# One stage for the mLSTM steps and the output projection, weight loads moved in the first stage, and a norm by a diagonal product

## The chip, the cores and the metric

One core of one Trainium2 chip. The time is the device time of one execution in microseconds; before the change the median of 3 runs is 1603.19 us (1601.73 to 1606.86). TensorE (PE) multiplies, VectorE (DVE), ScalarE (ACT) and GpSimd (POOL) do elementwise work, and SyncE (SP) issues the DMAs. A matmul keeps a stationary operand in the array, streams a moving operand past it and writes a bank of PSUM (8 banks of 512 f32 per partition).

## The reference, cut to what matters

One layer on 1024 prompt rows and 8 streams of 16 sample rows, 1152 rows of 1024 numbers in all:

```python
h = _rmsnorm(x, norm1)
gq, gk, gv, gr, glr, mq, mk, mv, mo, mi, mf = _split_proj(h @ w_in)
o_g = _head_rmsnorm(gla(gq, gk, gv, log_a), gla_norm) * silu(gr)      # 4 heads: half "a" of the mix
h_m = _head_rmsnorm(sigmoid(mo) * mlstm(mq, mk, mv, i, log_f), m_norm) # 4 heads: half "b" of the mix
x = x + concat([o_g, h_m]) @ w_out
y, conv_new = _conv_ffn(_rmsnorm(x, norm2), conv_st, w_g, w_u, conv_w, conv_b, w_d)
x = _rmsnorm(x + y, norm_f)
# _mlstm per chunk: num = qk@v + w*(q@C); den likewise; h = num/den; C = decay*C + k^T v (a recurrence over chunks)
```

## The kernel before

Rows go in 9 tiles of 128; the sample rows are tile 8. Large products are split in three: each f32 operand is written as hi + lo (f32r), and `mm3` (lines 91 to 95) adds hi*hi, lo*hi and hi*lo in one bank. ACT writes a weight's hi part by a copy, POOL its lo part by a subtraction; a weight comes in pieces of 128x1024 (512 KB). There are four stages, each with its own semaphores and a barrier behind it:

- `front` (0 to 494.7 us): norm 1, the input projection, and the GLA steps. `front_order` writes the order of the work out by hand, and every engine walks the same list: ("w", i) splits piece i, ("t", ...) and ("n", ...) are projection groups whose results go to DRAM, ("score", s), ("out", s), ("load", s) are a GLA step. Each projection group and GLA bank takes the next of 4 PSUM banks in a ring, and waits until that bank was emptied. SP issues in list order too: at ("w", i) it loads piece i + 2 into one of two raw slots, as soon as piece i is split, and every store and load behind it in the list waits along with it. `load` 2 brings the gate rows (`grin`, line 509) that DVE needs in `out` 2.
- `memory` (494.7 to 619): 8 prompt steps and then the sample step of the mLSTM. Per step PE transposes columns, multiplies q by k, then (when DVE has weighted that, `m_am`) the numerators, and the updates of the state C; DVE divides, and writes C; ACT sums squares. The step's inputs are loaded two steps ahead. The state makes each step wait for the one before. The halves of the mix go unscaled into `x9` (the GLA half loaded from DRAM, the mLSTM half by DVE).
- `output` (619 to 766.2): all head norms at once (`scale`, line 1468, on DVE and POOL), PE transposes of the mix (`Turn`, line 120), products with the 8 pieces of w_out, the residual added by DVE, and norm 2 (`Norm`: squares on ACT, a scaled copy `o_x_scaled` by DVE at line 185, transposed by PE at line 120). The transposed, normalised rows stay in `h2T_hi` and `h2T_lo`.
- `ffn` (766.2 to 1602.2): 11 pairs of 128 FFN columns, PE idle only before its first product and behind its last.

These lines say what a step before waits for:

```python
            def two_on(c, s):
                for n in ("am_ready", "qs_ready", "kt_ready"):
                    sp.wait_ge(g[n], c + 1)
                front(c + 2, s)
```

## Time and profile before

| | us |
|---|---|
| median of 3 runs | 1603.19 |
| the profiled execution | 1604.1 |
| its span | 1602.2 |
| PE busy | 1490.3 (93%) |
| DVE, ACT, POOL busy | 608.0, 438.7, 426.4 |
| mean granted clock of PE, share of full | 0.956 |

The span runs from the first to the last instruction. PEclk is the share of full speed that the clock throttle granted PE. A bracket behind a timeline row tells how long the engine was idle before it, and for whom it waited. SPq rows are DMA issues, not transfers. `m_` names belong to the mLSTM stage, `o_` to the output stage, `f_` to the FFN, `p_` to the first; `bank` is PSUM.

### The profile page before, as it was taken

How to read it: one execution, taken by the hardware profiler on the slowest of the kernel's cores; microseconds unless marked ns; L12 is line 12 of the kernel's file. 1: busy time of each engine (PE TensorE's matmuls, PEld its weight loads, DVE VectorE, ACT ScalarE, POOL GpSimd, SP SyncE). 2: the span in 40 equal slices, each digit the busy share in tenths (PEclk: the TensorE clock that was granted, in tenths of full speed). 3: DMA queues.
4: the chain of work that ended last, by engine and by line, in shares of the span. 5: the costliest groups of instructions: out<-in, count | busy, mean ns of one | idle time of the engine just before them, and what ended most of it. 6: DMA issues, size and time to landing. Idle time of an engine off the chain costs nothing.

```text
span 1602.2 us, 20822 instructions
## 1 busy us (share of the span) xinstructions
PE 1490.3 (93%) x7946; PEld 1359.7 (85%) x7946; DVE 608.0 (38%) x1189; ACT 438.7 (27%) x892; POOL 426.4 (27%) x356
## 2 busy tenths in 40 slices
PE   5999999989995785998899999999999999999997
PEld 5988878879995675776899898989899999989896
DVE  6352302545621436133233424243433333342426
ACT  5222222323311333132422131322232222213123
POOL 2312224254311223300431322313241313132220
PEclk9999999989996766999899999999999999999999
DMA  5312433232226733320210101111111101010103
GB/s 192 127 53 95 155 108 116 83 104 89 80 68 213 207 95 119 119 79 0 85 53 26 52 27 51 39 39 52 37 44 37 65 26 52 26 52 26 39 13 123
DMA packets 69329, 122.97 MB, mean 77 GB/s; under 512 B 5440, under 2 KB 40836, under 8 KB 68640
## 3 DMA queue, kind: packets, MB, share of 16 engines
q1 hardware_dynamic: 69280, 122.31, 22.7%
q8 instruction: 31, 0.51, 0.1%
q14 instruction: 18, 0.15, 0.0%
HBM read 93.65 MB, written 28.64 MB: 76 GB/s over the span
## 4 chain that ended last, share of the span: by engine, by line
PE 51%; DVE 1%; POOL 0%; ACT 0%; issue 0%; POOLq 0%
PE bank L93 17%; PE bank L94 17%; PE bank L95 17%; DVE x L1831 1%; DVE x L1812 0%; POOL f_w_lo L1670 0%; ACT f_w_hi L1692 0%; DVE f_inv L1824 0%; DVE f_ss L1822 0%; ACT f_rstd L1735 0%; POOLq L1663 0%; POOLq L1665 0%; POOLq L88 0%
## 5 line engine op out<-in xcount | busy, mean ns | idle before, releaser
L93 PE MATMUL bank<-h2T_hi,f_w_hi 128*128 128x384 f32 x1056 | 354.1, 335 | 6.7 <-POOL f_w_lo L1670 6.7
L94 PE MATMUL bank<-h2T_lo,f_w_hi 128*128 128x384 f32 x1056 | 353.9, 335 | 0.0
L95 PE MATMUL bank<-h2T_hi,f_w_lo 128*128 128x384 f32 x1056 | 353.8, 335 | 0.0
L1681 POOL TENSOR_TENSOR f_a_lo<-f_gate_conv,f_a_hi 128x384 fp32r<-128x384 f32 x66 | 67.0, 1015 | 579.9 <-ACT f_a_hi L1721 579.9
L93 PEld LDWEIGHTS bank<-h2T_hi,f_w_hi 128*128 128x128 f32 x1056 | 199.1, 189 | 7.4 <-POOL f_w_lo L1670 7.0
L94 PEld LDWEIGHTS bank<-h2T_lo,f_w_hi 128*128 128x128 f32 x1056 | 199.1, 189 | 0.4
L95 PEld LDWEIGHTS bank<-h2T_hi,f_w_lo 128*128 128x128 f32 x1056 | 199.1, 189 | 0.0
L1812 DVE TENSOR_TENSOR x<-bank,x 128x512 f32<-128x512 f32 x198 | 136.8, 691 | 126.0 <-PE bank L95 126.0
L1670 POOL TENSOR_TENSOR f_w_lo<-w_raw,f_w_hi 128x1024 fp32r<-128x1024 f32 x66 | 157.5, 2394 | 0.8 <-ACT f_w_hi L1692 0.8
L93 PE MATMUL bank<-f_w_hi,f_a_hi 128*128 128x512 f32 x396 | 154.4, 390 | 0.3
L95 PE MATMUL bank<-f_w_hi,f_a_lo 128*128 128x512 f32 x396 | 154.3, 390 | 0.0
L94 PE MATMUL bank<-f_w_lo,f_a_hi 128*128 128x512 f32 x396 | 154.3, 390 | 0.0
L1794 DVE TENSOR_SCALAR f_gate_conv<-f_gate_prompt,f_taps 128x384 f32<-128x384 f32 (+1 forms) x66 | 31.2, 473 | 298.2 <-ACT f_gate_prompt L1707 203.4
L93 PE MATMUL bank<-p_w_hi,p_h1T_hi 128*128 128x512 f32 x288 | 112.6, 391 | 3.6 <-POOL p_w_lo L545 3.6
L95 PE MATMUL bank<-p_w_hi,p_h1T_lo 128*128 128x512 f32 x288 | 112.1, 389 | 0.0
L94 PE MATMUL bank<-p_w_lo,p_h1T_hi 128*128 128x512 f32 x288 | 112.1, 389 | 0.0
L93 PE MATMUL bank<-p_h1T_hi,p_w_hi 128*128 128x384 f32 x312 | 106.7, 342 | 3.4 <-DVE p_h1T_lo L892 3.4
L545 POOL TENSOR_TENSOR p_w_lo<-p_raw,p_w_hi 128x1024 fp32r<-128x1024 f32 x29 | 69.8, 2413 | 148.5 <-ACT p_w_hi L601 148.3
L94 PE MATMUL bank<-p_h1T_lo,p_w_hi 128*128 128x384 f32 x312 | 105.7, 339 | 0.0
L95 PE MATMUL bank<-p_h1T_hi,p_w_lo 128*128 128x384 f32 x312 | 105.6, 338 | 0.0
L93 PEld LDWEIGHTS bank<-f_w_hi,f_a_hi 128*128 128x128 f32 x396 | 74.3, 188 | 16.9 <-DVE x L1812 1.6
L95 PEld LDWEIGHTS bank<-f_w_hi,f_a_lo 128*128 128x128 f32 x396 | 74.3, 188 | 15.5
(201 smaller groups left out, 2157.0 us busy)
## 6 DMA issues: line engine op xcount, KB each, us to landing
w_raw<-in_w SPq DMA_DIRECT2D x74, 512.0 KB, 3.3
p_raw<-in_w SPq DMA_DIRECT2D x29, 512.0 KB
scratch_pN<-p_n_out SPq DMA_DIRECT2D x36, 256.0 KB, 2.0
scratch_pT<-p_t_out SPq DMA_DIRECT2D x36, 192.0 KB, 1.9
p_arena<-in_x SPq DMA_DIRECT2D x9, 512.0 KB, 7.9
p_arena<-scratch_pN SPq DMA_DIRECT2D x18, 256.0 KB, 3.0
m_t_in<-scratch_pT SPq DMA_DIRECT2D x9, 512.0 KB
x<-in_x SPq DMA_DIRECT2D x9, 512.0 KB, 4.7
```

The lines of the kernel that those rows point to most:

```text
L93: pe.matmul(out, stat[0], mov[0], start=start, stop=False)
L94: pe.matmul(out, stat[0], mov[1], start=False, stop=False)
L95: return pe.matmul(out, stat[1], mov[0], start=False, stop=stop)
L545: pool.tensor_tensor(w_lo[:, i % NS_, :], raw[:, i % 2, :], w_hi[:, i % NS_, :].bitcast(F32), ALU.subtract).then_inc(g["piece_split"], 1)
L1670: pool.tensor_tensor(w_lo[:, unit, :], raw[:, slot, :], w_hi[:, unit, :].bitcast(F32), ALU.subtract).then_inc(piece_split, 1)
L1681: pool.tensor_tensor(a_lo[:, q, s], gc[:, n % 2, :], a_hi[:, q, s].bitcast(F32), ALU.subtract).then_inc(a_split, 1)
L1794: ins = dve.tensor_scalar(dst, src(2), tap[2], tap[3], ALU.mult, ALU.add)
L1812: dve.tensor_tensor(x, bank[6 + half], x, ALU.add).then_inc(down_added, 1)
L1831: dve.scalar_tensor_tensor(out=x9[:, r, :], in0=x9[:, r, :], scalar=rstd[:, r:r + 1], in1=raw[:, 0, :], op0=ALU.mult, op1=ALU.mult).then_i ...
```

## The change

The stages `memory` and `output` become one, `back`, over 9 steps, the sample tile first. Every step's head norm, transposes and products are done as soon as its inputs are there: ("a", s, half) adds the GLA half's product of step s to a 512-column half of x, ("b", s, half) the mLSTM half's; "a" runs one or two steps ahead. `back_order` is walked by every engine, and all 8 banks are one ring. POOL scales both halves and takes inverse roots by a power; the 9 tiles of x are loaded at the stage's start. The pieces of w_out 0 to 4 are split at the end of `front`, into the places of spent ones, and 5 to 7 and the FFN's first three in `back`. In `front` the load of a piece is an item of its own ("l", i), later in the list than before. Norm 2 has no scaled copy: the FFN stage multiplies x's 128x128 blocks as stationary operand by a diagonal matrix of inverse roots (f32), which transposes and scales at once; 36 of the 72 blocks before its first product, 36 between the first ones. (In `HALVES` the blocks of 3 row tiles are named by row block and column blocks.)

```diff
--- before.py
+++ after.py
...
-        front(nc, a, o, const, cols, ssq, pb, bank)
+        front(nc, a, o, const, cols, ssq, w, raw, pb, bank)
         x9 = sb("x9", [P, RT, D])
-        memory(nc, a, o, ident, x9, ssq, pb, bank)
-        hT = [sb(f"h2T_{n}", [P, KD, ROWS], F32R) for n in ("hi", "lo")]
-        raw = sb("w_raw2", [P, 4, PIECE])
-        output(nc, a, x9, ssq, cols, hT, ident, bank, raw)
-        ffn(nc, a, o, x9, hT, bank, raw)
+        back(nc, a, o, ident, cols, ssq, ssn, rstd2, w, raw, x9, bank)
+        ffn(nc, a, o, ident, cols, rstd2, w, raw, x9, bank)
...
-           + [PC_T + t for t in range(4, NT)])
+           + [PC_T + t for t in range(4, NT)] + [PC_OUT + j for j in range(5)])
+OUT_UNIT = W_ORDER.index(PC_OUT) % N_UNITS_W
+FFN_EARLY = 3
...
+    where = {i: sum(1 for x in order[:order.index(("w", i))] if x in units) for i in range(N_UNITS_W)}
+    before = [[] for _ in range(len(units) + 1)]
+    for i in range(N_UNITS_W, len(W_ORDER)):
+        n = last_use[i - N_UNITS_W]
+        shared = units[n][0] == "n" and (W_ORDER[i - N_UNITS_W] - PC_N) % 4 < 3
+        where[i] = min(max(n if shared else n + 1, where[i - 2] + 2, where[i - 1]), len(units))
+    for i in range(2, len(W_ORDER)):
+        before[min(where[i - 2] + (1 if i > 6 else 0), len(units))].append(("l", i))
+    for i in range(N_UNITS_W, len(W_ORDER)):
+        before[where[i]].append(("w", i))
...
-                if x[0] == "w" and x[1] + 2 < len(W_ORDER):
-                    load(x[1] + 2)
+                if x[0] == "l":
+                    load(x[1])
...
+def back_order():
+
+    dense = []
+    for s in range(RT):
+        dense += [[("a", s, 0)], [("a", s, 1)] + ([("turn_a", s + 2)] if s + 2 < RT else [])]
+    take = lambda n: [x for unit in [dense.pop(0) for _ in range(n)] for x in unit]
+    order = [("load", 0), ("load", 1), ("rows", 0), ("qk", 0), ("turn_a", 0), ("turn_a", 1)] + take(2)
+    order += [("w", 5), ("w", 6), ("num", 0)]
+    for b in range(NB):
+        order += [("um", 0, b)]
+        if b == 3:
+            order += [("w", 7), ("rows", 1), ("qk", 1)]
+    order += [("load", 2)] + take(2) + [("turn_b", 0)]
+    for s in range(1, RT):
+        order += [("num", s), ("um", s, 0)]
+        if s + 1 < RT:
+            order += [("rows", s + 1)]
+        order += [("b", s - 1, 0)]
+        if s + 1 < RT:
+            order += [("qk", s + 1)]
+        order += [("b", s - 1, 1)]
+        order += take(2) if dense else []
+        order += [("load", s + 2)] if s + 2 < RT else []
+        order += [("turn_b", s)]
+    order += [("ffn", m) for m in range(FFN_EARLY)] + [("b", RT - 1, 0), ("b", RT - 1, 1)]
+    return order
...
+            def load_step(s):
+                c, slot = GLA_STEPS[s], s % 2
                 r = slice(c * P, (c + 1) * P)
...
+                if s >= 2:
+                    wait_taken(sp, last_um(s - 2))
+                sp.dma_start(rin[:, slot, :, :], a["rows"][:, :, r]).then_inc(rows_in[slot], 16)
                 for dst, q in ((wt, 0), (wq, 2)):
...
+                    sp.dma_start(dst[:, slot, :, :], a["rows"][:, q, r].unsqueeze(0).to_broadcast([P, H, P]))\
+                      .then_inc(rows_in[slot], 16)
+                sp.dma_start(tin[:, slot, :, :], a["pT"][4:NT, :, r].rearrange("t p f -> p t f"))\
+                  .then_inc(tiles_in[slot], 16)
+                sp.dma_start(vin[:, slot, :, 0:DH], a["pN"][1, c].rearrange("p (h v) -> p h v", h=H))\
+                  .then_inc(v_in[slot], 16)
+                sp.dma_start(oin[:, slot, :], a["pN"][3, c]).then_inc(v_in[slot], 16)
+            def load_og(s):
+                sp.dma_start(ogin[:, s % 2, :], a["pN"][2, GLA_STEPS[s]]).then_inc(og_in[s % 2], 16)
...
+            load_step(0)
+            sp.dma_start(caus[:, 0:P], a["const"][:, C_CAUS:C_CAUS + P]).then_inc(g["const_in"], 16)
+            sp.dma_start(caus[:, P:3 * P], a["const"][:, C_ONE:C_ONE + 2 * P]).then_inc(g["const_in"], 16)
+            sp.dma_start(parity[:, :], a["const"][:, C_PARITY:C_PARITY + 2]).then_inc(g["const_in"], 16)
+            load_og(0)
+            load_og(1)
+            load_x(0)
+            sp.dma_start(C_s[:, :, :, :], a["s_mc"]).then_inc(g["state_in"], 16)
+            load_piece(0)
+            load_x(1)
+            load_piece(1)
+            load_step(1)
+            for s in range(2, RT):
+                load_x(s)
+            for x in order:
+                if x[0] == "turn_a" and x[1] + 2 < RT:
+                    wait_filled(sp, x)
+                    load_og(x[1] + 2)
+                elif x[0] == "load" and x[1] >= 2:
+                    load_step(x[1])
+                    if x[1] == 2:
+                        sp.dma_start(o["q_mc"], C_s[:, :, :, :]).then_inc(g["state_out"], 16)
+                elif x[0] in ("w", "ffn") and piece_at(x) + 2 < len(BW):
+                    load_piece(piece_at(x) + 2)
+            for n in range(2):
+                sp.wait_ge(g["piece_split"], len(BW) - 1 + n)
+                m = FFN_EARLY + (len(BW) + n) % 2
+                sp.dma_start(raw[:, (len(BW) + n) % 2, :], a["w"][PC_FFN + m]).then_inc(g["next_in"], 16)
...
+            def scale(x, rstd):
+                x = x.rearrange("p (h v) -> p h v", h=H)
+                return pool.tensor_tensor(x, x, rstd.unsqueeze(2).to_broadcast([P, H, P]), ALU.mult)
+
+            for x in order:
+                name, s = x[0], x[1]
+                if name == "load" and s == 0:
+                    masks(0)
+                elif name == "turn_a":
+                    if s == 0:
+                        pool.wait_ge(g["roots_a"], 1)
+                    pool.wait_ge(og_in[s % 2], 16 * (s // 2 + 1))
+                    scale(ogin[:, s % 2, :], rstd_a[:, GLA_STEPS[s], :]).then_inc(g["scaled_a"], 1)
+                elif name == "num":
+                    if s + 1 < RT:
+                        masks(s + 1)
+                    c = GLA_STEPS[s]
+                    pool.wait_ge(g["squared"], s + 1)
+                    pool.tensor_scalar(ssq[:, c, H:], ssq[:, c, H:], 1.0 / P, EPS, ALU.mult, ALU.add)\
+                        .then_inc(g["roots_step"], 1)
+                    pool.wait_ge(g["roots_step"], s + 2)
+                    pool.tensor_tensor(rstd_b[:, c, :], ssq[:, c, H:], power[:, 0:H], ALU.pow).then_inc(g["roots_b"], 1)
+                    pool.wait_ge(g["roots_b"], s + 1)
+                    scale(hm[:, s % 2, :], rstd_b[:, c, :]).then_inc(g["scaled_b"], 1)
...
+            def product(x, mix, turned, k0):
+                _, s, half = x
+                out = enter(x)
+                wait_taken(pe, (turned, s))
+                for k in range(H):
+                    j = k0 + k
+                    if s == 0 and half == 0 and j >= 5:
+                        pe.wait_ge(g["piece_split"], j - 4)
+                    stat = [y[:, s % 2, k, :] for y in mix]
+                    mov = [unit(j, y)[:, half * 512:(half + 1) * 512] for y in range(2)]
+                    mm = mm3(pe, out, stat, mov, k == 0, k == H - 1)
+                mm.then_inc(g["filled"], 1)
...
+            def turn(rb, ks):
+                if ks[0] == 0:
+                    pe.wait_ge(diag_ready, rb * JR + JR)
+                for k in ks:
+                    n = rb * KD + k
+                    if rb:
+                        pe.wait_ge(lo_done, n - 3)
+                    for j in range(JR):
+                        r = rb * JR + j
+                        t = pe.matmul(turn_bank(rb, k)[:, j * P:(j + 1) * P], x9[:, r, k * P:(k + 1) * P],
+                                      diag[:, r, :], start=True, stop=True)
+                    t.then_inc(turned, 1)
...
+                            if first and m == 0:
+                                pe.wait_ge(lo_done, KD * (rb + 1))
+                            up(i, q, rb, m)
+                            if first and rb < 2 and (rb, m) != (1, 1):
+                                turn(*HALVES[2 + 2 * rb + m])
...
+            turn(*HALVES[0])
+            turn(*HALVES[1])
+            pairs(pe, body)
```

The three places that matter below, in the order that the programs have. On SP in `front`, where pieces 25 to 28 are loaded (`p_raw`, `w_raw`), before:

```order
L440 DMA p_raw<-in_w 128x1024 x3
L478 DMA scratch_pN<-p_n_out 128x512
L440 DMA p_raw<-in_w 128x1024
L473 DMA scratch_pT<-p_t_out 128x384
L506 DMA scratch_pN<-p_arena 128x512
L509 DMA p_arena<-scratch_pN 128x512
```

and after:

```order
L491 DMA scratch_pN<-p_n_out 128x512 x3
L453 DMA w_raw<-in_w 128x1024 x2
L486 DMA scratch_pT<-p_t_out 128x384
L519 DMA scratch_pN<-p_arena 128x512
L522 DMA p_arena<-scratch_pN 128x512
L466 DMA p_arena<-scratch_pN 128x512
```

Two of four piece loads, and the waits that go with them, no longer stand ahead of the gate rows' load (L509 before, L522 after).

On PE, one mLSTM step before (updates of C, then the next step's q by k, columns, transposed keys, then its numerators):

```order
L1324 MATMUL bank4<-m_v_in,m_ks 128x129 x4
L1276 MATMUL bank2<-m_t_in 128x128 x4
L1282 MATMUL bank0<-ident,m_r_in 128x4 x3
L1283 MATMUL bank0<-m_dg,m_const 128x4
L1286 MATMUL bank2<-ident,m_t_in 128x128 x4
L1310 MATMUL bank6<-m_C_prompt,m_qs 128x129
L1311 MATMUL bank6<-m_v_in,m_am 128x129
```

and the same place after (the triple at L93 to L95 comes four times in each of the step's four half products):

```order
L1489 MATMUL bank0<-m_v_in,m_ks 128x129 x4
L1435 MATMUL bank2<-ident,m_r_in 128x4 x3
L1436 MATMUL bank2<-m_dg,m_caus 128x4
L1441 MATMUL bank2<-ident,m_t_in 128x128 x4
L93 MATMUL bank4<-w_hi,m_mix_b_hi 128x512
L94 MATMUL bank4<-w_lo,m_mix_b_hi 128x512
L95 MATMUL bank4<-w_hi,m_mix_b_lo 128x512
```

48 product matmuls of 512 columns now lie between one step's updates and the next step's numerators, 12 of them before q by k.

On SP at the start of `back` (from the sample state's load; `m_og_in` is the GLA half of a step, and the last row holds those of steps 2, 3 and 4):

```order
L1266 DMA m_C_sample<-in_s_mc 128x4128
L1234 DMA w_raw<-in_w 128x1024
L1256 DMA x<-in_x 128x1024
L1234 DMA w_raw<-in_w 128x1024
L1241 DMA m_r_in<-scratch_rows 4x5x128
L1243 DMA m_wt<-scratch_rows 128x4x128
L1243 DMA m_wq<-scratch_rows 128x4x128
L1245 DMA m_t_in<-scratch_pT 128x8x128
L1247 DMA m_v_in<-scratch_pN 128x4x128
L1249 DMA m_o_in<-scratch_pN 128x512
L1256 DMA x<-in_x 128x1024 x7
L1252 DMA m_og_in<-scratch_pN 128x512 x3
```

In the stage before, SP issued two steps' inputs, the state, nine loads of 256 KB (the GLA halves, into x), and then the third step's inputs:

```order
L1194 DMA m_C_sample<-in_s_mc 128x4128
L1196 DMA x<-scratch_pN 128x512 x9
L1172 DMA m_t_in<-scratch_pT 128x8x128
L1173 DMA m_r_in<-scratch_rows 4x5x128
L1175 DMA m_wt<-scratch_rows 128x4x128
```

The seven late tiles of x (512 KB each) now stand between step 1's inputs and the GLA half of step 2.

And on the same queue from step 1 on, after:

```order
L1252 DMA m_og_in<-scratch_pN 128x512
L1241 DMA m_r_in<-scratch_rows 4x5x128
L1243 DMA m_wt<-scratch_rows 128x4x128
L1243 DMA m_wq<-scratch_rows 128x4x128
L1245 DMA m_t_in<-scratch_pT 128x8x128
```

A step's inputs are behind an `m_og_in` load, which waits until PE has filled a transpose ("turn_a").

## Rows read from the trace of the kernel before

**Rows 1.** Busy time by stretch: length, each engine's busy us, PEclk, DMA share, GB/s
```profile
0.00:494.70 494.70, 460.00 (x2506) 405.94 (x2506) 193.51 (x359) 146.87 (x268) 150.35 (x193) 0.98 0.31 104
494.70:619.00 124.30, 85.31 (x508) 78.58 (x508) 46.12 (x184) 31.48 (x145) 25.30 (x21) 0.65 0.57 177
619.00:766.20 147.20, 122.07 (x576) 100.61 (x576) 58.16 (x91) 45.42 (x79) 28.37 (x9) 0.94 0.20 72
766.20:1602.20 836.00, 822.87 (x4356) 774.56 (x4356) 310.23 (x555) 214.89 (x400) 222.38 (x133) 0.99 0.14 46
```

**Rows 2.** Waits of PE from 494 to 770.5 us: us in total, times, longest
```profile
PE bank L1310 <- DVE m_am L1360: 17.8, 8, 4.2
PE bank L1276 <- DMA m_wq<-scratch_rows: 16.2, 2, 14.5
PE bank L120 <- DVE x L1468: 11.8, 1, 11.8
PE bank L93 <- POOL f_w_lo L1670: 6.7, 1, 6.7
```

**Rows 3.** Timeline of POOL and DVE, 618 to 640 us
```profile
620.67 2.93 POOL L1468 TENSOR_TENSOR x<-x,o_rstd 128x1024 f32<-128x1024 f32 x1 [36.13 <-ACT o_rstd L1487]
627.93 2.37 POOL L1476 TENSOR_TENSOR o_w_lo<-w_raw,o_w_hi 128x1024 fp32r<-128x1024 f32 x1 [4.33 <-ACT o_w_hi L1483]
631.69 8.90 POOL L1476 TENSOR_TENSOR o_w_lo<-w_raw,o_w_hi 128x1024 fp32r<-128x1024 f32 x1 [1.39 <-ACT o_w_hi L1483]
...
631.51 6.89 DVE L1468 TENSOR_TENSOR x<-x,o_rstd 128x1024 f32<-128x1024 f32 x6
```

**Rows 4.** DMA from 506 to 526 us: all, and one issue (KB, us to landing)
```profile
DMA packets 5486, 6.73 MB, mean 337 GB/s; under 512 B 282, under 2 KB 4050, under 8 KB 5356
...
m_C_sample<-in_s_mc SPq DMA_DIRECT2D x1, 2064.0 KB, 10.2
```

**Rows 5.** Stretches of PE: in a product of 512 columns, and the sample's numerators
```profile
719.50:724.50 5.00, 5.00 (x23) 1.00 0.03 13
593.00:599.40 6.40, 6.36 (x73) 0.58 0.00 0
```

**Rows 6.** Timeline of DVE: two updates of the sample state
```profile
601.34 2.15 DVE L1389 SCALAR_TENSOR_TENSOR m_C_sample<-m_C_sample,m_col,bank 128x129 f32<-128x129 f32 x8
```

**Rows 7.** Timeline of PE in an mLSTM step
```profile
546.63 0.39 PE L1310 MATMUL bank<-m_C_prompt,m_qs 128*128 128x129 f32 x2
...
547.08 1.06 PE L1324 MATMUL bank<-m_v_in,m_ks 128*128 128x129 f32 x8
```

**Rows 8.** Timeline of SP and POOL: the last load of an mLSTM step, and its landing
```profile
537.04 0.51 SPq L1175 DMA_DIRECT2D m_wq<-scratch_rows  x1
...
541.80 1.26 POOL L1218 TENSOR_TENSOR m_wt<-m_wt,m_const 128x512 f32<-128x512 f32 x1 [6.49 <-DMA m_wq<-scratch_rows]
```

**Rows 9.** Timeline of PE: start us, us, engine line op [idle before <-releaser]
```profile
335.39 0.70 PE L826 MATMUL bank<-p_arena 64*128 64x128 f32 x2 [2.67 <-ACT p_n_out L700]
...
348.07 2.08 PE L779 MATMUL bank<-p_arena 128*128 128x256 f32 x4 [5.15 <-DVE p_arena L1040]
349.94 2.77 PE L772 MATMUL bank<-p_arena 128*128 128x128 f32 x12
...
396.06 1.03 PE L779 MATMUL bank<-p_arena 128*128 128x256 f32 x4
```

**Rows 10.** Stretches behind the FFN's first product at 770.2 us
```profile
770.00:773.00 3.00, 2.80 (x9) 2.80 (x10) 0.00 (x0) 0.00 (x0) 3.00 (x3) 0.50 0.55 175
...
776.00:779.00 3.00, 3.00 (x19) 3.00 (x19) 0.00 (x0) 1.66 (x2) 1.15 (x1) 1.00 0.70 229
```

**Rows 11.** The page, DMA issues: KB each, median us to landing
```profile
w_raw<-in_w SPq DMA_DIRECT2D x74, 512.0 KB, 3.3
```

**Rows 12.** Timeline of SP, the queue of the DMA issues, 330 to 342 us
```profile
330.57 7.06 SPq L440 DMA_DIRECT2D p_raw<-in_w  x3
...
341.16 0.43 SPq L509 DMA_DIRECT2D p_arena<-scratch_pN  x1
```

More of the change, by code:

```diff
@@ L1104, in _, with back_entries, back @@
                     take_outputs(x[1])
-def memory(nc, a, o, ident, x9, ssq, pb, bank):
-    SLOTS = 2
-    C0 = 4
+def back_order():
[23 more added lines that the diff above has]
+    return order
+def back_entries(order):
+    out = []
+    for x in order:
+        if x[0] in ("a", "b", "turn_a", "turn_b", "qk"):
+            out.append((x, "dve"))
+        elif x[0] == "rows":
+            out += [(x, "dve"), (("kt", x[1]), "act")]
+        elif x[0] in ("num", "um"):
+            out += [(x + (i,), "dve") for i in range(2)]
+    return out
+def back(nc, a, o, ident, cols, ssq, ssn, rstd2, w, raw, x9, bank):
+    order = back_order()
+    ring = Ring(back_entries(order), bank)
     with ExitStack() as ctx:
@@ new lines, in back, with wait_taken, wait_filled @@
+        last_um = lambda s: ("um", s, (NB if s == 0 else 1) - 1, 1)
+        block = ctx.enter_context(nc.Block())
+        def wait_taken(eng, name):
+            owner, n = ring.taken(name)
+            eng.wait_ge(taken[owner], n)
+        def wait_filled(eng, name):
+            eng.wait_ge(g["filled"], ring.filled(name))
+        g["filled"] = sem("filled")
+        turns = [x for x in order if x[0] in ("turn_a", "turn_b")]
+        BW = [5, 6, 7] + [PC_FFN - PC_OUT + m for m in range(FFN_EARLY)]
@@ L1289, in from_states, with enter @@
[L1289 to L1301 removed]
+            def enter(name):
+                before = ring.before(name)
+                if before:
+                    pe.wait_ge(taken[before[0]], before[1])
+                return ring.bank(name)
@@ new lines, in _ @@
+            pe.wait_ge(g["cleared"], CLEARED)
+            for x in order:
+                name = x[0]
+                if name == "rows":
+                    rows(x[1])
+                elif name == "qk":
+                    products(x[1])
+                elif name == "num":
+                    numbers(x[1])
+                elif name == "um":
+                    updates(x[1], x[2])
+                elif name == "turn_a":
+                    turn(x, ogin, "scaled_a")
+                elif name == "turn_b":
+                    turn(x, hm, "scaled_b")
+                elif name == "a":
+                    product(x, mix_a, "turn_a", 0)
+                elif name == "b":
+                    product(x, mix_b, "turn_b", H)
@@ L1400, in masks @@
                 q.then_inc(g["qm_ready"], 1)
-            def front(v, c, s):
-                diagonal(v, c, s)
-                columns(v, c, s)
-                weights(v, c, s)
-            def step(vb, vf, c, s):
-                diagonal(vf, c + 1, 1 - s)
-                hidden(vb, c, s)
-                states(vb, c, s)
-                columns(vf, c + 1, 1 - s)
-                weights(vf, c + 1, 1 - s)
-                if vf.sample:
-                    masks(c + 1, 1 - s)
-            def back(v, c, s):
-                hidden(v, c, s)
-                states(v, c, s)
@@ L1595, in ffn @@
+def ffn(nc, a, o, ident, cols, rstd2, w, raw2, x9, bank):
     NP = NF // 2
```

772 lines of the change are left out of this document (361 added, 411 removed).

## The prediction

> **What bounds the kernel now.** I read busy time by stretch first [rows 1]. In `front` and in the FFN TensorE is busy 93% and 98% of the time at a clock near full, so little can be won there. In `memory` it is busy 85.3 of 124.3 us at a mean granted clock of 0.65, and in `output` 122.1 of 147.2: 64 idle microseconds, and much of the busy time at 1.2 GHz instead of 2.4. The waits say why [rows 2]: 16.2 us for a step's inputs, 14.5 of them at the stage's start; 17.8 us in eight waits for `m_am`, a chain over ACT and DVE in every step with nothing beside it; 11.8 us from the end of `memory` over a barrier and the scaling to the first transpose; 6.7 us before the FFN's first product. The work of `memory` is a chain, that of `output` is dense: the change puts one beside the other.
>
> The sum is made against the profiled execution, 1604.1 us with a span of 1602.2, which is 0.9 above the median of 1603.19. What it replaces runs from 494.7 us (SP's first load of `memory`) to 770.2 (the FFN's first product): 275.5 us. I price the new path between the same two events, stretch by stretch, in TensorE's order.
>
> **Opening of `back`: 41 us.** Until the GLA half of step 2 is there, TensorE has transposes of steps 0 and 1 and one step's products, 24 matmuls. Those are over at about +30. The inputs land near +12: before it was +9.7, SP now waits a good microsecond for POOL's clearing, and the masks stand behind more loads. POOL's two mask operations, sample keys and two scalings of 512 columns (half of 2.93 us each, [rows 3]) take until +20, the products 8 to 10 us at the low clock. Then PE, POOL and ACT all have "turn_a" of step 2 ahead of the sample's numerators. Its load stands behind all that the order shows: two steps' inputs (1546 KB each), constants 193, two GLA halves 512, the state 2064, two pieces 1024, nine tiles of x 4608, together 11.5 thousand KB or 11.8 MB. At the measured mean of 337 GB/s [rows 4] that is 35 us; with 3 to 4 us of start, the half itself and its scaling, the transpose starts at +41. This takes loads of one queue to land about in issue order; the state's 10.2 us to landing, for 6 us of data at that rate, with two steps' loads just issued, is such a backlog. Bounds: +30 if the small load passes the others, +48 at 280 GB/s.
>
> **Sample step: 26 us.** Numerators 6.3 us, as at 593 to 599.3, mean clock 0.58 [rows 5]; DVE's division and eight state updates, 8 x 1.08 [rows 6], 11 together, since with eight banks TensorE need not wait for DVE after each; columns and weights of step 1 on DVE 2 to 3, and the rest of step 1's products some 6 us later. DVE and the low clock set this; 20 to 30.
>
> **Seven full steps: 117 us.** At full clock a 512-column matmul comes every 0.227 us (22 periods in 5 us, [rows 5]), an mLSTM product in two passes every 0.225 (two in 0.45, [rows 7]). Per step: 48 x 0.227 = 10.9, numerators 8 x 0.225 = 1.8, updates 0.9, q by k 0.9, columns and keys 1.4, two rounds of transposes 1.0: 16.9 us. Seven are 118, less 1 for two that have one round. The chains are covered: in `memory` all of DVE's work is 46.12 / 9 = 5.1 us a step, ACT's 3.5, POOL's 2.8 [rows 1]; even all three and a scaling of 1.5 end to end are 13, and TensorE has 15 us of other work between numerators and "turn_b". So the 17.8 us go, and what is late next is a load.
>
> **Late inputs: 23 us.** From step 1 on SP loads a step's inputs behind an `m_og_in` load that waits for a "turn_a" of PE. That transpose is the last thing but one of a step, and the next step needs the inputs for its columns after only 3.2 us (turn_b, numerators, updates). From the issue of the last of them, `m_wq`, to POOL's start it took 4.8 us [rows 8]; with the other load, rows and wt issued ahead (1.7 us) and the keys' 512 KB behind them, the transposed keys start at about +9: 9 - 3.2 - 0.6 = 5.2 us lost. Queued behind them is all else of PE's step. SP waits so for "turn_a" 4, 5 and 6, ahead of loads 3, 4 and 5; later loads have no such wait. Three times 5.2 is 15.6. A wait of 2.67 us was enough to bring the clock down [rows 9]: at 348 us four 256-column matmuls took 2.08 us against 1.03 at 396. From 770.2 the clock was at half for the first 3 us, full from 776 [rows 10]: some 5 us of work at half speed, so 2.5 us for each wait, 7.5. Bounds 0 (loads land in 3 us) and 40 (every step).
>
> **Last step 9, tail 16, opening of the FFN 12.5.** Step 8 has numerators 1.8, updates 0.9, half products of step 7 5.4, turn_b and its wait 0.9: 9. From there PE needs 7 us for its last products, but the weights take longer: ACT and POOL split the pieces ffn 0, 1, 2 only now, 2.4 us each on POOL [rows 3], the third is loaded once the first is split, 3.3 us to landing [rows 11], and SP ends the stage when the piece that it loads behind the last split has landed: 0.8 + 1.1 + 2.4 + 3.3 + 1.1 + 2.4 + 3.4 = 14.5, and the barrier. So PE idles 10 us and starts at 1.2 GHz. POOL builds diagonals (1.9); then 24 products with them, two passes like the `m_ks` row, eight passes in 0.9 [rows 7], so 0.22 us each at full clock and 0.43 at half: 8 us, and 12 more in 2.6. Together 12.5.
>
> Sum: 41 + 26 + 117 + 23 + 9 + 16 + 12.5 = 244.5, 31 less than 275.5.
>
> **In the FFN: +5.** The other 36 diagonal products cost 36 x 0.22 = 7.9 us on the critical engine; what ACT and DVE do with them lies beside the up products, and costs up to 5 if it does not. The engine is at full clock at its first product, which gives back about 2.8 [rows 10]. The copies `o_x_scaled` go at no gain beyond the 275.5.
>
> **In `front`: -9.** At 335 us TensorE waited 2.67 us because ACT, held at piece 25, had not emptied a bank, and until 348 another 5.15 for DVE, which had no gate rows [rows 9]: SP issued them only at 341.2, after three piece loads that held it from 330.6 to 337.6, and a fourth [rows 12]. Now two piece loads stand ahead, the gate rows go out at about 334, 7 us earlier, and the bank is free. With part of the low clock (until 352.7) this gives 9; bounds 0 and 13. Five more splits, 12 us of POOL and 5 of ACT, find POOL busy 150 of 494.7 us [rows 1]: no cost, and up to 3 if one stands ahead of a key.
>
> Total: -31 + 5 - 9 = -35: **1569 us**.
>
> **Two rules weighed.** Clock: the rows show it fall after 2.67 us idle, and a half clock for some 5 us behind 770.2. The Trainium skill, TensorE: Matmul & The Clock Gate, section HAM oscillation, tells of a kernel in which every burst starts cold because a wait for a transfer stands between bursts. By that rule the three late steps cost what I charged if the clock recovers within them, and the second rival if it doesn't; the trace agrees as far as that a short wait brings it down. POOL: one subtraction took 8.90 us against 2.37, beside 6.9 us of DVE's two-operand scaling [rows 3]. The Trainium skill, GPSIMD Engine Reference, section Specifications, has POOL share its way to SBUF with VectorE, in contention when VectorE has two SBUF inputs; the trace agrees. That DVE work is gone in `back`, where most of what DVE reads is one operand from PSUM, so POOL keeps its times; by the rule alone its lone operations could be anything up to 3.8 times longer, which is the third rival.
>
> **Rivals.** *The loads don't bind* (0.16): the half of step 2 passes or the queue runs at 400 GB/s, and the steps' inputs land in time. That gives back 11 and 23: 1535; one of the two alone 1546 to 1558. For it: 4050 of the 5486 packets behind the 337 GB/s were under 2 KB [rows 4], and the tiles of x come in larger ones. Against: these loads are 11.8 MB, and all must pass. *The clock stays low in the mixed steps* (0.05), the case that ends slower: at half clock a step costs 15 us more, and the gain of 35 is gone after 2.3 such steps; seven make 1674. For it: three waits of 5 us, and 0.65 in `memory`. Against: `front` mixes such small matmuls with large ones at 0.98 [rows 1]. *POOL becomes the bound* (0.07): its 2.8 us of masks, 1.4 of roots and 2.9 of two scalings make 7 of 16.9 us; trebled by contention they cost 4 us in each of seven steps: 1597. *The change doesn't overlap what it should* (0.02): the ring of banks ties products to DVE's adds, a step takes 22 us, and 5 x 7 takes the 35 back: 1604.
>
> **Numbers.** The forecast has 0.70, own range 1554 to 1585 (opening 7, late inputs 10, front 4 either way). The range with the neighbours is 1540 to 1595. A measurement of this kernel can tell 0.3%, 5 us. Faster by more 0.93 (forecast, loads, POOL), within 0.02 (the last case), slower 0.05 (the clock).
>
> **What would show it.** On the new stage's PE timeline: a wait of about 10 us ahead of turn_a of step 2, behind `m_og_in`; three waits of 4 to 6 us at the columns or keys of steps 3, 4 and 5, behind `m_wq` or `m_t_in`, none at 6 to 8; steps of 17 us otherwise; 10 us idle before the diagonal products; `front` ending near 486. It is wrong if PE waits for `m_am` or the scaled hidden rows, if PEclk in the seven steps is near 0.5, or if the sample's numerators start at +30.

## The result, and the profile after

The changed kernel takes 1610.86 us in the median of 14 runs (1607.66 to 1615.11), the kernel before, now also in 14 runs, 1605.71 (1597.91 to 1610.12): a ratio of 1.0038, 95% interval 1.0024 to 1.0052. Forecast were 1569 us and a range of 1540 to 1595; the change is 0.4% slower.

The profiled execution has a span of 1613.3 us, 11.1 more than before. It is the slowest of the 14, 4.3 us over their median, and the medians are only 5.2 us apart: some of the misses below may belong to this one execution. Its stretches, cut where the prediction cut them: `front`; the opening of `back` until the transposes of step 2; the sample step; the seven full steps; last step, tail and first diagonal products; the FFN. They answer to [rows 1]. The columns are those of that group, with the count of instructions in brackets.

```profile
0.00:498.60 498.60, 462.78 (x2506) 408.42 (x2506) 197.63 (x360) 151.88 (x273) 162.54 (x201) 0.97 0.32 109
498.60:540.30 41.70, 15.23 (x52) 12.17 (x52) 5.40 (x11) 3.67 (x10) 13.74 (x8) 0.58 0.87 295
540.30:575.60 35.30, 29.30 (x185) 24.84 (x185) 16.65 (x48) 7.11 (x20) 12.91 (x10) 0.64 0.29 87
575.60:736.10 160.50, 136.97 (x701) 117.28 (x700) 56.68 (x168) 41.35 (x139) 38.25 (x40) 0.87 0.29 82
736.10:775.80 39.70, 25.33 (x151) 22.55 (x149) 13.66 (x30) 13.90 (x28) 16.65 (x18) 0.83 0.22 66
775.80:1613.30 837.50, 828.52 (x4431) 780.05 (x4429) 320.59 (x570) 193.45 (x392) 215.48 (x129) 1.00 0.13 44
```

The first number of a row after its borders is its length. Set beside the terms of the sum:

| stretch | predicted | measured | miss |
|---|---|---|---|
| start of the new stage, against 494.7 before | -9 | +3.9 | 12.9 |
| opening | 41 | 41.7 | 0.7 |
| sample step | 26 | 35.3 | 9.3 |
| seven full steps with late inputs | 117 + 23 | 160.5 | 20.5 |
| last step, tail, opening of the FFN | 9 + 16 + 12.5 | 39.7 | 2.2 |
| FFN from its first product, against 832.0 before | +5 | +5.5 | 0.5 |

So the 46 us between -35 and +11 are nearly all in three places: `front`, the sample step, the seven steps. TensorE's waits in the new stage, the answer to [rows 2], name the one in the steps. The first row is longest at 5.7 us, but comes eight times:

```profile
PE bank L1435 <- DVE m_dg L1544: 29.0, 8, 5.7
PE bank L1435 <- DMA m_parity<-in_const: 18.2, 1, 18.2
PE bank L1498 <- POOL m_og_in L1324: 13.6, 2, 12.9
PE bank L1820 <- POOL f_diag L1718: 11.4, 1, 11.4
```

`m_am`, 17.8 us before, is gone as forecast, and TensorE does not wait for the hidden rows in the full steps. In its place it waits before the columns of every step (L1435) for `m_dg`, the 4 by 4 decay matrix that one VectorE multiplication of 0.15 us makes. Two engines' timelines of one step show why:

```profile
673.86 1.06 PE L1489 MATMUL bank<-m_v_in,m_ks 128*128 128x129 f32 x8
677.23 0.80 PE L1435 MATMUL bank<-ident,m_r_in 4*128 4x4 f32 x6 [2.31 <-DVE m_dg L1544]
...
673.88 0.34 DVE L1567 COPY m_den<-bank 128x2 f32<-128x2 f32 x2
674.86 1.12 DVE L1574 SCALAR_TENSOR_TENSOR m_hidden<-bank,m_den,m_o_in 128x128 f32<-128x128 f32 x4
675.90 1.12 DVE L1587 SCALAR_TENSOR_TENSOR m_C_prompt<-m_C_prompt,m_col,bank 128x129 f32<-128x129 f32 x4
676.93 0.14 DVE L1544 TENSOR_TENSOR m_dg<-m_r_in,ident 4x4 f32<-4x4 f32 x1
```

The multiplication needs only the next step's gate rows, which were there. But it stands in VectorE's queue behind the denominators, the hidden rows and the state update, and TensorE's queue goes from the update straight to the columns: nothing covers the 2.31 us. After the wait TensorE is at half clock for a while; from numerators to numerators this step takes 21.1 us.

Steps 3 to 5 have that, and late rows besides. SyncE issues them only behind an `m_og_in` load that waited for TensorE, and VectorE is through with its queue at 626.8:

```profile
621.63 0.33 SPq L1252 DMA_DIRECT2D m_og_in<-scratch_pN  x1
622.01 0.64 SPq L1241 DMA_DIRECT2D m_r_in<-scratch_rows  x1
623.17 0.51 SPq L1243 DMA_DIRECT2D m_wq<-scratch_rows  x1
...
630.16 0.15 DVE L1544 TENSOR_TENSOR m_dg<-m_r_in,ident 4x4 f32<-4x4 f32 x1 [3.33 <-DMA m_wq<-scratch_rows]
```

### The profile page after: what moved, and what is told of

It is laid out like the page before. It is cut to its first block, busy times and chain, and to the rows that moved or that the text cites. A ratio compares the mean times of both kernels' runs of the same rounds, so it can differ in the third digit from the quotient of the medians.

```text
span 1613.3 us, 20932 instructions
## 1 busy us (share of the span) xinstructions
PE 1498.1 (93%) x8018; PEld 1365.3 (85%) x8018; DVE 610.6 (38%) x1185; ACT 411.4 (25%) x861; POOL 459.6 (28%) x405
## 4 chain that ended last, share of the span: by engine, by line
PE 51%; DVE 1%; POOL 0%; issue 0%; ACT 0%; POOLq 0%
PE bank L93 17%; PE bank L95 17%; PE bank L94 17%; PE bank L1820 1%; DVE x L1928 0%; DVE x L1909 0%; POOL f_diag L1718 0%; ACT w_raw L1804 0%; DVE f_inv L1921 0%; DVE f_ss L1919 0%; ACT f_rstd L1796 0%; POOLq L1714 0%; POOLq L1716 0%; POOLq L88 0%
## 5 line engine op out<-in xcount | busy, mean ns | idle before, releaser
L93 PE MATMUL bank<-f_h2T_hi,w_hi 128*128 128x384 f32 x1056 | 353.3, 335 | 0.1
L95 PE MATMUL bank<-f_h2T_hi,w_lo 128*128 128x384 f32 x1056 | 352.9, 334 | 0.0
L94 PE MATMUL bank<-f_h2T_lo,w_hi 128*128 128x384 f32 x1056 | 352.9, 334 | 0.0
L93 PEld LDWEIGHTS bank<-f_h2T_hi,w_hi 128*128 128x128 f32 x1056 | 198.2, 188 | 0.7 <-issue 0.4
L94 PEld LDWEIGHTS bank<-f_h2T_lo,w_hi 128*128 128x128 f32 x1056 | 198.2, 188 | 0.4
L95 PEld LDWEIGHTS bank<-f_h2T_hi,w_lo 128*128 128x128 f32 x1056 | 198.2, 188 | 0.0
L93 PE MATMUL bank<-w_hi,f_a_hi 128*128 128x512 f32 x396 | 154.4, 390 | 0.4 <-DVE x L1909 0.2
L95 PE MATMUL bank<-w_hi,f_a_lo 128*128 128x512 f32 x396 | 154.3, 390 | 0.0
L94 PE MATMUL bank<-w_lo,f_a_hi 128*128 128x512 f32 x396 | 154.3, 390 | 0.0
L558 POOL TENSOR_TENSOR w_lo<-w_raw,w_hi 128x1024 fp32r<-128x1024 f32 x34 | 82.0, 2422 | 183.5 <-ACT w_hi L614 183.5
L93 PE MATMUL bank<-w_hi,p_h1T_hi 128*128 128x512 f32 x288 | 113.2, 393 | 5.4 <-POOL w_lo L558 5.4
L95 PE MATMUL bank<-w_hi,p_h1T_lo 128*128 128x512 f32 x288 | 112.7, 391 | 0.0
L93 PE MATMUL bank<-p_h1T_hi,w_hi 128*128 128x384 f32 x312 | 106.5, 341 | 3.1 <-DVE p_h1T_lo L905 3.1
L1723 POOL TENSOR_TENSOR w_lo<-w_raw,w_hi 128x1024 fp32r<-128x1024 f32 x42 | 100.7, 2398 | 22.7 <-ACT w_hi L1744 22.7
L95 PE MATMUL bank<-p_h1T_hi,w_lo 128*128 128x384 f32 x312 | 105.5, 338 | 0.0
L93 PEld LDWEIGHTS bank<-w_hi,f_a_hi 128*128 128x128 f32 x396 | 74.4, 188 | 16.8 <-DVE x L1909 1.0
```

Source lines behind the costliest of these rows:

```text
L93: pe.matmul(out, stat[0], mov[0], start=start, stop=False)
L94: pe.matmul(out, stat[0], mov[1], start=False, stop=False)
L95: return pe.matmul(out, stat[1], mov[0], start=False, stop=stop)
L558: pool.tensor_tensor(w_lo[:, i % NS_, :], raw[:, i % 2, :], w_hi[:, i % NS_, :].bitcast(F32), ALU.subtract).then_inc(g["piece_split"], 1)
L1723: pool.tensor_tensor(w_lo[:, unit, :], slots[slot], w_hi[:, unit, :].bitcast(F32), ALU.subtract).then_inc(piece_split, 1)
```

## The experiments

All ratios are to the kernel before on the same chip; the changed kernel's is 1.0038. "Steps" are the seven times from one step's numerators to the next one's, from the profile; the changed kernel has 21.1, 24.3, 26.2, 24.0, 21.1, 22.2, 20.7.

| kernel | median us | ratio, 95% interval | steps, us |
|---|---|---|---|
| e1_decay_first | 1586.4 | 0.987 (0.983 to 0.991) | 17.2, 23.9, 26.1, 24.1, 17.2, 16.8, 16.8 |
| e2_load_first | 1600.0 | 0.9971 (0.995 to 0.9991) | 21.1, 21.1, 22.7, 21.1, 21.1, 22.2, 20.7 |
| e3_opening | 1599.7 | 0.9969 (0.9946 to 0.9991) | 23.4, 24.3, 26.5, 24.3, 21.1, 22.2, 20.7 |
| e4_all | 1555.8 | 0.9686 (0.965 to 0.9721) | 17.2 five times, 16.8 twice |
| e5_pool_front | 1537.5 | 0.9583 (0.9564 to 0.9602) | as e4 |
| e6_tail | 1557.1 | 0.9714 (0.9698 to 0.9731) | as e4 |
| e7_transposes | 1549.8 | 0.9675 (0.9659 to 0.9691) | as e4 |
| e8_front_loads | 1554.0 | 0.9693 (0.967 to 0.9715) | as e4 |
| e9_rows_later | 1588.0 | 0.9901 (0.9871 to 0.9931) | 18.2, 21.1, 22.8, 20.4, 18.2, 19.4, 17.7 |
| e10_rows_and_loads | 1582.0 | 0.9873 (0.983 to 0.9915) | 18.2, 19.8, 18.2, 19.8, 19.8, 17.8, 19.3 |

**e1_decay_first.**

```diff
                 elif name == "num":
+                    if s + 1 < RT:
+                        decays(s + 1)        # m_dg, taken out of columns(s + 1)
                     hidden(s)
```

> The small multiplication on VectorE that makes the decay matrix of the next step (m_dg) is put ahead of the hidden rows and the state update on VectorE's queue; nothing else moves. Theory (queue place): TensorE waits before the columns of every step because this multiplication stands behind 2.3 us of other VectorE work. Where the step's rows are in on time (steps 2, 6, 7, 8: idle 2.31 us each) the wait goes, and with it about 1.5 us of half clock behind it, 4 x 3.8 = 15 us; at step 1 the wait of 5.5 us goes as well. Sum -20 us, a ratio to the changed kernel of 0.988. In steps 3, 4, 5 the wait stays at 2.5 to 3.5 us, for the rows are late there. Rival (the wait only moves: to a bank, to the keys, or to the masked scores): idle of the same length in front of another line, ratio 0.998 to 1.000. Rival (clock): the half clock behind the columns is not a consequence of the idle time; the waits go and the steps still last 18.5 us, ratio 0.993.

By the ratios 1.7% were won, 27 us. The four steps whose rows are in time lost the wait and the half clock with it; the three late ones kept theirs, as TensorE's waits in the new stage show:

```profile
PE bank L1435 <- DVE m_dg L1544: 14.2, 3, 5.7
```

So the order of VectorE's queue was the cause of these waits, and in the full steps the half clock was their consequence. Both rivals fall: nothing took the wait's place, and the steps went to 17.2, not 18.5. The sample step went from 35.3 to 27 us, which is why more was won than the 20 us expected.

**e2_load_first.** `("load", s + 2)` directly behind `("um", s, 0)` in the order, instead of behind the products with `turn_a` s + 3.

> SyncE issues the inputs of step s+2 right behind the state update of step s, ahead of the attention rows of step s+5, whose load waits for TensorE; nothing else moves on the engines that compute. Theory (late issue): the rows of steps 3, 4 and 5 were late by 3.3, 2.5 and 1.3 us over the place in VectorE's queue; the waits before the columns fall from 4.82, 5.74 and 3.73 us to 2.31 each, -7.4 us, with the clock that comes back -9, ratio to the changed kernel 0.9945. Rival (the transfer itself is slow, 8 us from issue to landing): same waits, ratio 1.000.

The same row of the waits:

```profile
PE bank L1435 <- DVE m_dg L1544: 21.7, 8, 5.5
```

The eight waits sum to 21.7 us instead of 29.0, -7.3; seven of them are now at 2.31, the other is the sample step's. Late issue, not slow transfer, made these steps late.

**e3_opening.** Constants loaded before step 0's inputs; `load_x(2)` moved behind the attention rows of step 2, `load_x(3)` to `load_x(8)` behind those of step 3.

> On SyncE the constants are loaded ahead of the inputs of step 0, and the tiles 2 to 8 of x behind the attention rows of steps 2 and 3 instead of ahead of them. Theory (backlog of the queues): the constants land 4 us sooner (-3 us), and the attention rows of step 2 land near 525 us and not 539, so that the wait of 12.9 us goes and some 4 us of it come back as a wait for the three weight pieces or the sample states. Sum -11 us, ratio to the changed kernel 0.993. Rival (the sample states or the pieces, which stand ahead of both in the queue, bind as late): -3 us, ratio 0.998. Rival (x now comes late for its additions): a new wait of VectorE for x, ratio 1.000 to 1.003.

From the end of `front` on TensorE to the transposes of step 2 it is 37.3 us, 47.6 in the changed kernel. The GLA half of step 2 still comes 6.1 us late: ahead of them stand step 1's inputs, the state and two pieces. VectorE never waits for x. By the ratios -11 us, as expected.

**e4_all**, the three together.

> The three edits together: the decay multiplication first on VectorE, inputs of step s+2 first on SyncE, and the constants and attention rows ahead of x in the opening. Theory: with the rows in on time the 2.3 us and the half clock behind it go in all seven steps, 27 us, with 5 us in the sample step, 5 to 7 us of lateness and 11 us in the opening: -45 us, about 1565 us, steps of 17 us as the prediction had them. Rival (the edits remove waits that lie behind one another, so that the next chain binds, such as rows of POOL or the masked scores): -20 us or less.

Better than expected: -3.5%, 56 us, where the three alone give 49. Each of the late steps carried both causes; the queue's 2.31 us and its clock could only go there once the rows were early. TensorE's rows by stretch (borders as above, without the FFN):

```profile
488.70:526.50 37.80, 14.37 (x52) 11.48 (x52) 6.23 (x12) 4.16 (x11) 14.95 (x11) 0.64 0.79 266
526.50:556.70 30.20, 29.20 (x185) 25.07 (x186) 15.02 (x48) 7.12 (x20) 13.81 (x10) 0.65 0.57 204
556.70:676.00 119.30, 119.30 (x694) 102.85 (x693) 55.35 (x167) 41.16 (x139) 37.73 (x40) 1.00 0.39 108
676.00:716.80 40.80, 26.18 (x156) 23.18 (x155) 13.83 (x30) 13.88 (x28) 16.69 (x18) 0.83 0.22 64
```

In the seven steps (third row) TensorE is busy all of 119.3 us at full clock, against the 117 that the prediction added up from matmul counts. The sample step (second row) is 30.2 us here, not e1's 27: its wait is gone as well, but the low clock lasts longer.

**e9_rows_later and e10_rows_and_loads** hide the wait in TensorE's order instead of VectorE's. e10 adds e2's edit.

```diff
-        if s + 1 < RT:
-            order += [("rows", s + 1)]
         order += [("b", s - 1, 0)]
         if s + 1 < RT:
-            order += [("qk", s + 1)]
+            order += [("rows", s + 1), ("qk", s + 1)]
```

> The changed kernel with one swap in the written order, on all engines: the columns and keys of step s+1 stand behind the first half product of step s-1 and no longer ahead of it; VectorE's queue still has the decay multiplication behind the hidden rows and the state update. Theory (TensorE has nothing between the update and the columns that covers VectorE's 2.3 us): the half product of 3.2 us covers it, so the waits of 2.31 us go and those of 4.82, 5.74 and 3.73 us shrink to 1.6, 2.5 and 0.5; -19 us, with the clock -24, ratio to the changed kernel 0.985. The sample step keeps its 5.5 us, since its order is not touched. Rival (columns later make the masked scores late for the next numerators): a new wait for m_am of 1 to 3 us in each step, and -10 us or less.

> The swap of e9_rows_later and the early issue of e2_load_first. Theory: the 4.6 us of lateness that e9 leaves go too, all seven steps take 17.2 us as in e4_all although VectorE's queue is as in the changed kernel; -30 us, ratio to the changed kernel 0.981. Rival (the order of VectorE's queue matters by itself, for the state update or the scores): steps of 18 us or more, -24.

Both won, e9 22 us and e10 26, but e10's steps are not 17.2: its rival was right. Timelines of one step of e10:

```profile
630.94 0.80 PE L1433 MATMUL bank<-ident,m_r_in 4*128 4x4 f32 x6 [0.93 <-DVE m_dg L1542]
632.45 1.92 PE L1446 MATMUL bank<-m_t_in 128*128 128x128 f32 x8
...
630.05 0.69 DVE L1629 TENSOR_TENSOR x<-bank,x 128x512 f32<-128x512 f32 x1 [0.72 <-PE bank L95]
630.65 0.14 DVE L1542 TENSOR_TENSOR m_dg<-m_r_in,ident 4x4 f32<-4x4 f32 x1
```

The swap also moved the multiplication on VectorE, behind the addition of the very half product that was to cover it. VectorE waits for that product's end, adds, and only then makes `m_dg`: 0.93 us remain in every step.

**e5_pool_front**, on top of e4: GpSimd puts off `lower_exponents` until the splits that stand directly behind it in the order are done.

```diff
+                if x[0] in ("score", "out", "load", "zero", "n", "t") and later:
+                    lower_exponents(later.pop())
...
                     if x[1] + 2 < RT:
-                        lower_exponents(x[1] + 2)
+                        later.append(x[1] + 2)
```

> On top of the three edits of e4_all, in front and on GpSimd alone: where two splits of weight pieces follow the gate work of a step, GpSimd does the splits first and then the lower exponents of the step after next (eight operations, 3.5 us). Theory (front gained nothing because its waits hang on GpSimd's order, not on the order of the loads): at 201 us TensorE waits 4.7 to 5.4 us for a w_lo that stands behind these eight operations, and at 342 us 3.5 us for a bank, since the next pieces are loaded only after the splits that stand behind them. Both waits go (-8.5 us) and the half clock behind each (-3 and -2.5): -14 us against e4_all's 1555.8, so 1542. Rival (the exponents are needed as soon as the splits): the wait comes back at the masked products of the attention, L1053 on VectorE; 0 to +5 us. Rival (the loads, not the splits, are late): the first wait goes, the second stays, -7.

GpSimd at 200 us in e4, and in e5, where eight operations (L584, L587) and two splits (L558) have changed places:

```profile
199.60 2.94 POOL L584 TENSOR_TENSOR p_arena<-p_arena 128x128 f32<-128x128 f32 x7 [2.27 <-DVE p_arena L974]
202.50 0.61 POOL L587 TENSOR_TENSOR p_arena<-p_arena 128x256 f32<-128x256 f32 x1
203.07 4.67 POOL L558 TENSOR_TENSOR w_lo<-w_raw,w_hi 128x1024 fp32r<-128x1024 f32 x2
```

```profile
196.46 4.95 POOL L558 TENSOR_TENSOR w_lo<-w_raw,w_hi 128x1024 fp32r<-128x1024 f32 x2 [0.21 <-ACT w_hi L617]
202.93 2.95 POOL L584 TENSOR_TENSOR p_arena<-p_arena 128x128 f32<-128x128 f32 x7 [1.52 <-DVE p_arena L977]
205.84 0.61 POOL L587 TENSOR_TENSOR p_arena<-p_arena 128x256 f32<-128x256 f32 x1
```

What TensorE waited for in `front` after 60 us in e4, three rows; and `front` in e5 from 86.4 us on (from 60 us it waits for nothing either):

```profile
PE bank L93 <- POOL w_lo L558: 4.7, 1, 4.7
PE bank L799 <- ACT p_t_out L720: 3.5, 1, 3.5
PE bank L792 <- DVE p_arena L1053: 2.6, 2, 1.4
```

```profile
86.40:475.90 389.50, 389.50 (x2135) 341.53 (x2134) 167.32 (x301) 118.73 (x220) 136.62 (x178) 0.99 0.32 104
```

TensorE is busy for all of 389.5 us, and `front` ends at 476.0 instead of 488.7. The third kind of wait, 2.6 us that I had not counted, went as well. The 12.7 us are more than the scatter of `front` told of below (its earliest end elsewhere is 484.9), and the ratios give about 16.5. e5 is the fastest version found, 4.2% faster than before.

**e8_front_loads**: `before[min(where[i - 2], len(units))].append(("l", i))`, without the one product of delay.

> On top of e4_all, in front: each weight load stands at the place of the split two pieces before it, as in the kernel before, and no longer one product behind it. Theory (SyncE waits for that split in either place): same waits at 201 and 342 us, time within 2 us of e4_all. Rival (the later place is what kept the gate rows back or forward, as the prediction had it): the stall at 342 us grows from 3.5 to 8 us or more, +5 to +9 us.

1554.0 against 1555.8 us. The three kinds of wait shown for e4 above sum to 12.1 us here and to 10.8 there, the one at 342 us is 3.7 and 3.5: this delay of the loads gains and costs nothing.

**e6_tail**, on top of e4: `("ffn", 0), ("ffn", 1)` before `("num", 8)`, `("ffn", 2)` behind `("turn_b", 8)`.

> On top of e4_all: the pieces ffn 0 and 1 are split ahead of step 8 and ffn 2 behind its second round of transposes, instead of all three at the end. Theory (the tail is held by the third split): the last sum of squares no longer stands behind the split of the third piece, so the root and the stage's end come 2.3 us sooner, and TensorE waits 9.3 us before the first diagonal product instead of 11.6: -2.3 us. Rival (the stage ends when SyncE's last piece has landed): that load is issued sooner too, same sign, down to -4. Rival (the two early splits delay GpSimd's scaling of the last hidden rows): the wait of 3.0 us before the last products grows by up to 2 and nothing is gained.

Nothing gained; the last rival was right. The wait for the diagonals fell by 3.9 us (11.6 in e4), but only because TensorE ended its last product 4.7 us later, counted from the numerators of step 8: GpSimd's two splits now stand ahead of the scaling of the last hidden rows. From the numerators of step 8 to the first diagonal product it is 30.0 us, 29.3 in e4. TensorE's waits in this stretch:

```profile
PE bank L1828 <- POOL f_diag L1726: 7.7, 1, 7.7
PE bank L1499 <- POOL m_hidden L1325: 3.5, 1, 3.5
PE bank L93 <- DVE m_mix_b_lo L1628: 1.7, 1, 1.7
```

**e7_transposes**, on top of e4: `pe.transpose(..., x9[...], ident)` for the product with `diag`. This kernel leaves out the row factor of norm 2, so it only prices the products.

> On top of e4_all: the 72 products with a diagonal matrix become plain transposes of x. This leaves out the row factor of the second norm; the diagonals are still built and waited for. Theory (an f32 product of 128 columns takes 0.22 us, two passes, a transpose 0.11): 72 x 0.11 = 8 us at full clock, 10 with the first 12 at half clock; the -8 us split into about -4.5 before the first product of the FFN and -4 behind it. Rival (what follows on ScalarE and VectorE, 0.58 and 0.62 us a chunk, sets the pace of the three late groups): -3 to -5.

From the first of these operations to the end of the span it is 842.0 us, 847.9 in e4: -5.9. The three late groups of twelve took 1.47 us each instead of 2.84 and the opening 3.5 less, 7.6 together. Some 2 were lost again to two waits for VectorE's `f_h2T_lo` (1.8 and 0.2 us) that e4 doesn't have; that is the rival's mechanism, in small. The comparison of medians can't tell this size well (the ratios are 0.1% apart, well within e4's interval).

## Why the prediction was wrong, by its steps

**Seven full steps, 117 us: the arithmetic was right, the claim of cover wrong.** The sum of 16.9 us a step is what e4 shows, 16.8 to 17.2. "The chains are covered" failed: I compared the length of the chains, 13 us end to end, with the 15 us of other TensorE work between numerators and "turn_b". But TensorE takes its queue in order, and the columns of the next step stand there with nothing between them and the update. The cover has to be counted between the instruction that starts a chain and the one that waits for it, and the chain includes whatever VectorE has queued ahead, which the row of 2.15 us for eight operations [rows 6], half of it for a step's four, would have warned of, and the denominators and hidden rows besides. In a step whose rows are in time it cost 2.3 us and, with the half clock behind it, some 4. The seven steps took 159.6 us, 119.6 in e4; of the 40.0 between them, late inputs alone make 22.5 (e1) and the queue alone 30.5 (e2). A late step waits only for what ends last, so the two don't add up. The prediction had the first and not the second: this failed step is 17.5 of the 20.5 us missed here.

**Late inputs, 23 us: right.** Steps 3, 4 and 5, behind `m_og_in`, as forecast. In the changed kernel the waits there were 4.8, 5.7 and 3.7 with the queue's share under them; in e1, without it, 4.5, 5.7 and 4.0 where 5.2 each were forecast, and with the half clock the three steps take 22.5 us more than in e4. The step's inputs took 7 us from the issue of `m_wq` to VectorE, not 4.8 [rows 8].

**Sample step, 26: failed, 35.3.** The same queue: 5.52 us before the columns of step 1, where sixteen operations of the state update, 4.2 us, stand ahead of the multiplication, which then takes 2.08 us instead of 0.15 beside a split of GpSimd (last section). e1 alone brought it to 27. The low clock of the second 32 update matmuls, 6.55 us, was not in the sum.

**Front, -9: failed; the step named the wrong queue.** The two piece loads that now stand ahead of the gate rows each wait for a split, and GpSimd gave these only at 337.6 and 339.9 us, after its exponents; the gate rows went out at 341.2 as before. Rows of the changed kernel:

```profile
337.56 2.65 SPq L453 DMA_DIRECT2D w_raw<-in_w  x2
341.20 0.49 SPq L522 DMA_DIRECT2D p_arena<-scratch_pN  x1
...
331.66 2.95 POOL L584 TENSOR_TENSOR p_arena<-p_arena 128x128 f32<-128x128 f32 x7 [2.53 <-DVE p_arena L974]
335.15 4.70 POOL L558 TENSOR_TENSOR w_lo<-w_raw,w_hi 128x1024 fp32r<-128x1024 f32 x2
...
345.65 0.66 PE L799 MATMUL bank<-ident,p_arena 128*128 128x128 f32 x2 [3.66 <-ACT p_t_out L720]
```

I had read SyncE's row of 7.06 us for three loads [rows 12] as loads in the way, and had not asked what each load waited for. The two waits that were to go, 2.67 and 5.15 us, did become one of 3.66, but e8, with the loads in their former places, has that too (3.7), so the loads' places are not the reason. And what was gained there was lost elsewhere: at 201 us TensorE waited 5.4 us where it had waited 3.6 in two waits, with half clock behind it, and behind 357 us 2.5 where it had waited for nothing. All waits of `front` after 60 us are 11.6 us, 11.4 before. e8 shows that moving the loads changes nothing, e5 that moving GpSimd's work gives 13 us. `front` also varies by itself: with the same program it ended on TensorE at 492.7, 491.8, 491.0, 487.0, 488.7, 484.9 and 488.0 us in the changed kernel, e1 to e4, e6 and e7, and at 489.9 before. The change gained nothing here, and +3.9 is within that scatter.

**Opening 41, opening of the FFN 12.5, FFN +5: right.** The wait for `m_og_in` of step 2 was 12.9 us where about 10 were named, and e3 confirms the backlog. The diagonal products cost +5.5 in the FFN, and e7 gets back 5.9 with the opening.

**Tail 16: right in its path, 2.3 us short.** From the last "turn_b" to the first diagonal product it is 20.2 us, where 16 and 1.9 were priced. GpSimd's first split starts 3.1 us behind "turn_b" and not 1.9, and the third piece took 4.1 us from issue to ScalarE, not 3.3. The root comes behind the third split and ends at 760.25, but SyncE's last piece, issued at that split's end too, still moves until 761.0. GpSimd waits 3.13 us at the barrier here, and 1.77 in e6 (last row), where that piece was loaded long before. No run moved the piece alone:

```profile
755.74 2.34 POOL L1351 TENSOR_TENSOR w_lo<-w_raw,w_hi 128x1024 fp32r<-128x1024 f32 x1 [2.89 <-ACT w_hi L1417]
758.46 1.79 POOL L1355 TENSOR_TENSOR rstd<-ssn,m_power 128x9 f32<-128x9 f32 x1
763.38 2.93 POOL L1718 TENSOR_SCALAR f_diag<-ident,rstd 128x128 f32<-128x128 f32 x5 [3.13 <-POOLq L88]
...
700.34 5.24 POOL L1726 TENSOR_SCALAR f_diag<-ident,rstd 128x128 f32<-128x128 f32 x9 [1.77 <-POOLq L88]
```

**The rivals.** The end was on the side of the last one: steps of 22 us, so that "the change doesn't overlap what it should", at 0.02 and 1604 us. Its mechanism, the ring of banks, was not the one. The low clock did not stay: behind each wait in the seven steps it came back within the step, so the price of 15 us a step never applied. I left 0.02 and 0.05 for everything beyond the rows that I had thought of; the order of one queue was enough.

Left open: why `front` ends up to 8 us apart in executions of one program, and what lowers the clock in the sample step (last section).

## What to carry to other kernels

When a chain is said to be hidden, find in the waiting engine's queue the instruction that starts it and the one that needs it, and count only the work between the two; then add to the chain all that its own engines have queued ahead. A tiny operation that needs only early inputs belongs ahead of the long ones in its queue. Before a load is moved, ask what it waits for at its place: here both stalls in `front` were decided on GpSimd, and the change of SyncE's order that e8 took back had not touched them.
